# Mamba decay rows and their selection matrix: 64 contraction rows against 128, the added rows zero

## What is computed

```python
def _ssd_chunk(state, xs, A):
    x, dt, Bc, Cc = xs
    Q = x.shape[1]
    causal = jnp.tril(jnp.ones((Q, Q), dtype=bool))
    a = jnp.cumsum(dt * A, axis=1)
    seg = jnp.where(causal[None, :, :, None, None], a[:, :, None] - a[:, None, :], -jnp.inf)
    w = jnp.einsum('btgn,bsgn->btsg', Cc, Bc)[..., None] * jnp.exp(seg) * dt[:, None]
    y = jnp.einsum('btsgh,bsghp->btghp', w, x) + ...
```

## Time and profile before

| | |
|---|---|
| median of 3 runs | 1443.24 us (1440.71 to 1446.42) |
| span of the profiled execution, first to last instruction | 1436.6 us |
| own time of the profiled execution beside its span | not recorded |
| TensorE busy | 1412.7 us, 98% |
| VectorE busy | 1013.4 us, 71% |
| ScalarE busy | 719.4 us, 50% |
| GpSimd busy | 85.1 us, 6% |
| mean granted TensorE clock | 0.995 |
| DMA | 337.41 MB, 235 GB/s |

### The profile page before, as it was taken

One profiled execution on the slowest core, in us unless ns is written; L12 is line 12 of the kernel. 1 busy time (PEld: TensorE's weight loads), 2 busy tenths in 40 slices (PEclk: granted clock), 3 DMA queues, 4 the chain that ended last, 5 costly groups with the idle time before them and its releaser, 6 DMA issues.

```text
span 1436.6 us, 18540 instructions
## 1 busy us (share of the span) xinstructions
PE 1412.7 (98%) x7578; PEld 1205.4 (84%) x7578; DVE 1013.4 (71%) x1278; ACT 719.4 (50%) x931; POOL 85.1 (6%) x112
## 2 busy tenths in 40 slices
PE   9999999998999999999999999999999999999997
PEld 8788888987888878888789978788888799999886
DVE  5887776987977769777767965678746544653865
ACT  5544456456544365434566676554345645545433
POOL 1000001001000010000100352100000100000000
PEclk9999999999999999999999999999999999999999
DMA  9887865855978849887544412488755454445542
GB/s 384 358 335 296 334 227 192 320 187 201 390 295 314 311 151 347 308 322 300 201 147 164 175 60 88 176 333 337 282 194 201 147 194 174 147 164 189 186 153 116
DMA packets 51396, 337.41 MB, mean 235 GB/s; under 512 B 6720, under 2 KB 9584, under 8 KB 11376
## 3 DMA queue, kind: packets, MB, share of 16 engines
q1 hardware_dynamic: 51312, 336.23, 62.8%
HBM read 335.12 MB, written 1.09 MB: 234 GB/s over the span
## 4 chain that ended last, share of the span: by engine, by line
PE 87%; DVE 5%; ACT 3%; DMA 2%; issue 1%; POOL 1%; SPq 0%; ACTq 0%; POOLq 0%; DVEq 0%
PE ps L1010 84%; DMA raw<-units 2%; PE ps L1228 1%; DVE wlo L1642 1%; DVE hf L2056 1%; ACT whi L537 1%; PE ps L1119 1%; DVE M L1652 0%; ACT hf L618 0%; POOL base L457 0%; PE ps L1491 0%; POOL ssx L458 0%; DVE xlo L1717 0%; DVE wlo L1647 0%; ACT hf L612 0%
## 5 line engine op out<-in xcount | busy, mean ns | idle before, releaser
L1642 DVE TENSOR_TENSOR wlo<-raw,whi 128x2048 fp32r<-128x2048 f32 x212 | 485.4, 2294 | 206.6 <-ACT whi L537 206.3
L1010 PE MATMUL ps<-whi,xhi 128*128 128x512 f32 x1432 | 568.7, 397 | 7.5 <-DVE wlo L1647 1.7
L1010 PE MATMUL ps<-whi,xlo 128*128 128x512 f32 x1432 | 558.7, 390 | 0.0
L1010 PE MATMUL ps<-wlo,xhi 128*128 128x512 f32 x1432 | 558.5, 390 | 0.0
L537 ACT ACTIVATE whi<-raw 128x2048 fp32r<-128x2048 f32 x218 | 416.7, 1914 | 157.5 <-DMA raw<-units 157.5
L1010 PEld LDWEIGHTS ps<-whi,xhi 128*128 128x128 f32 x1432 | 269.3, 188 | 69.7 <-issue 5.3
L1010 PEld LDWEIGHTS ps<-whi,xlo 128*128 128x128 f32 x1432 | 269.1, 188 | 57.8
L1010 PEld LDWEIGHTS ps<-wlo,xhi 128*128 128x128 f32 x1432 | 269.5, 188 | 52.7 <-issue 0.2
L1010 PE MATMUL ps<-xhi,whi 128*128 128x256 f32 x704 | 202.7, 288 | 0.0
L1010 PE MATMUL ps<-xhi,wlo 128*128 128x256 f32 x704 | 199.9, 284 | 0.0
L1010 PE MATMUL ps<-xlo,whi 128*128 128x256 f32 x704 | 199.8, 284 | 0.0
(11 more groups left out here) (238 smaller groups left out, 981.4 us busy)
## 6 DMA issues: line engine op xcount, KB each, us to landing
raw<-units SPq DMA_DIRECT2D x218, 1024.0 KB, 4.9
M<-ada_units SPq DMA_DIRECT2D x82, 1024.0 KB, 7.0
M<-units SPq DMA_DIRECT2D x10, 1024.0 KB, 5.0
gp<-gate_rows SPq DMA_DIRECT2D x7, 512.0 KB, 7.3
M<-cvec SPq DMA_DIRECT2D x2, 512.0 KB, 4.5
x<-x_in SPq DMA_DIRECT2D x1, 1024.0 KB, 6.0
ada_a<-ada_units SPq DMA_DIRECT2D x1, 1024.0 KB, 18.5
ada_b<-ada_units SPq DMA_DIRECT2D x1, 1024.0 KB, 22.4
```

Of the source, the lines that this page charges most:

```text
L1010: return pe.matmul(out, lhsT, rhs, start=start, stop=stop, skip_group_check=True)
L1642: dve.tensor_tensor(rest(u), landed(u), rounded(u).bitcast(F32), ALU.subtract).then_inc(w_lo, 1)
```

## The change

`sel` and `arows` get 128 partitions instead of 64. GpSimd sets both to zero at the start, behind its other constants, and each memset adds 1 to `const`, so that TensorE's and VectorE's waits go to 6. VectorE's writes into rows 0 to 63 stay as they are. The matmuls of `decay` take all 128 rows; rows 64 to 127 add zero. Lines behind 442 of the kernel move down by 2.

```diff
--- before.py
+++ after.py
@@ -124,8 +124,8 @@
         mask = sb("mask", [P, SEQ])
         ident16 = sb("ident16", [P, P], BF16)
         mask16 = sb("mask16", [P, P], BF16)
-        sel = sb("sel", [2 * H_MB, H_MB], F32R)
-        arows = sb("arows", [2 * H_MB, SEQ], F32R)
+        sel = sb("sel", [P, H_MB], F32R)
+        arows = sb("arows", [P, SEQ], F32R)
         ps = ctx.enter_context(nc.psum_tensor("ps", [P, 8, 512], F32))
 
         def m(off, *shape):
@@ -440,6 +440,8 @@
             step(pool.memset(mask[:, :], 0.0))
             pool.affine_select(out=mask[:, 0:P], in_=mask[:, 0:P], compare_op=ALU.is_ge, fill=NEG, base=0,
                                pattern=[[1, P]], channel_multiplier=-1).then_inc(S["const"], 1)
+            pool.memset(sel[:, :].bitcast(F32), 0.0).then_inc(S["const"], 1)
+            pool.memset(arows[:, :].bitcast(F32), 0.0).then_inc(S["const"], 1)
 
             taken = {}
 
@@ -1144,7 +1146,7 @@
 
             pe.wait_ge(S["const"], 1)
             keep_clock(7, 28)
-            pe.wait_ge(S["const"], 4)
+            pe.wait_ge(S["const"], 6)
             pe.wait_ge(S["rows_in"], 16)
             for a in range(4):
                 r = pe.transpose(ps[:, 6, a * P:(a + 1) * P], vrow[:, a, :], ident[:, :])
@@ -1407,7 +1409,7 @@
                         for j in range(2):
                             h = 2 * p + j
                             mm(ps[:, 2 + p % 2, j * SEQ:(j + 1) * SEQ],
-                               sel[:, h:h + 1].to_broadcast([2 * H_MB, P]), arows[:, :], start=(j == 0))
+                               sel[:, h:h + 1].to_broadcast([P, P]), arows[:, :], start=(j == 0))
                         masked(p, 0).then_inc(S["mb_ab"], 1)
 
                     def masked(p, t):
@@ -1941,7 +1943,7 @@
                         dve.scalar_tensor_tensor(out=e[:, SEQ:384], in0=q[:, P:SEQ], scalar=colm[:, 1, h:h + 1],
                                                  in1=mask[:, 0:P], op0=ALU.add, op1=ALU.min).then_inc(S["ml_arg"], 1)
 
-                    dve.wait_ge(S["const"], 4)
+                    dve.wait_ge(S["const"], 6)
                     for h in range(H_ML):
                         exponent(h)
                     lo(u0 + 10)
```

## The result

| | before | changed |
|---|---|---|
| median | 1440.35 us (8 runs) | 1437.19 us (8 runs) |
| lowest to highest | 1438.98 to 1446.42 | 1435.84 to 1438.75 |
| ratio | | 0.9968, 95% interval 0.9956 to 0.9981 |
| span of the profiled execution | 1436.6 us | 1434.1 us |
| its own time | not recorded | 1435.84 us, 1.7 above the span |

What follows compares the result with a forecast made beforehand. TensorE, busy nearly the whole span, was taken to bound the kernel only where it is last waited for: 0.27 + 0.60 + 0.90 + 0.30 = 2.07 us off 1443.24 gives 1441.2 us; own range 1439 to 1443.5, with rivals 1437.0 to 1445.6.

Steps and rivals of the forecast that it cites:

- The delay of a pair: Decay pair in the Mamba loop, first mask to heads: 0.77 us falls to 0.45 to 0.48, taken as 0.30 saved.
- No cost of more rows, of the memsets and of the waits: Zero rows priced at 0; two start memsets and longer waits covered, 0 taken, +0.62 us at most.
- The pairs on the path: Of 16 decay pairs, those where TensorE carries the chain were counted: 2.07 us out of 4.80.
- The term of 0.27 for the first two pairs: Two pairs at 808: would give 0.60, counted 0.27 because VectorE had been idle only that long.
- The 0.90 for 847 to 861: TensorE's path from 847.51 to 861.17: three pairs ahead of the mask matmul that frees ScalarE, 0.90 us.
- a longer wait near 847: Sign in the profile after: TensorE waits more for VectorE near 847, where three pairs gain 0.
- The 0.60 for 831 to 847: Two pairs between 831.02 and 839.59 gain 0.60 us; three more, up to 846.5, gain 0.
- a rival of 3.35 us on either side of the forecast: One more clock fall, 1444.5 us, chance 0.11; or the recorded fall near 875 absent, 1437.8 us, chance 0.07.
- The direction I argued: From 861 to 876 a faster TensorE stands still more, up to 0.3 us a turn, which could tip another clock fall.
- The base: Start from the runs' median of 1443.24 us, 6.6 us above the profiled span, that part taken as unchanged.
- What can be told from no change: Whole kernel: a measurement can tell about 0.5%, 7.2 us; faster 0.04, slower 0.02, the same 0.94.
- Heads after 875: Test of the path: heads starting over 3.5 us or under 1 us earlier would make the path wrong.

Runs made afterwards that it cites:

- the two without falls: Profiles of the kernel before and the changed kernel, each with small products added in three TensorE waits of the loop; ratios 0.9977 and 0.9966.
- r_before: The kernel before, unchanged, timed against itself and profiled a second time; ratio 1.0005.
- ten pairs: Against the kernel before, only the ten decay pairs predicted as covered take 128 rows, the other six keep 64; ratio 0.9999.
- two pairs: Against the kernel before, only the 4th and 5th of 16 decay pairs take 128 rows; ratio 1.0006.
- 96 rows: The changed kernel with decay matmuls reading 96 of the 128 rows; ratio 0.9973 against the kernel before.
- six pairs: Against the kernel before, only the 4th, 5th, 9th, 10th, 11th and 14th decay pairs take 128 rows; ratio 0.9975.
- row maximum too: The changed kernel with the mLSTM stage's eight 4-row matmuls also filled to 128 rows from a zeroed tile; ratio 0.9976 against before.
- products in the waits: Kernel before and changed kernel, each with small products of ones added in three TensorE waits of the loop; means 1438.9 and 1437.2 us.
- forty matmuls of 64 and of 128 rows: The kernel before with forty extra matmuls in a row at two places of the third gated MLP; medians 1459.3 (64 rows) and 1458.8 us (128).
- the burst with 64 changes: The kernel before with 64 extra matmuls in the third gated MLP, alternating 64 and 128 rows; 1470.55 us, against 1454.39 with all 128.

## Why the prediction was right or wrong

- **The delay of a pair** was right: 0.29 us predicted by the steps (0.30 taken), 0.77 to 0.48 measured. The rule of the Trainium skill, TensorE: Matmul & The Clock Gate, Part 3 (What overlaps and what doesn't), that a load overlaps only in another row group did not hold here: the 128-row load of the pair starts with the mask matmul of 128 rows ahead of it.
- **No cost of more rows, of the memsets and of the waits** was right: a ratio of 1.0008 for the memsets and waits alone, and steps of 0.12 us with 128 rows.
- **The pairs on the path** were right as a set, and too high by a fifth in the sum: 1.61 us in the two profiles, 1.67 in the two without falls and 1.7 ± 0.9 in their runs, against 2.07. The term of 0.27 for the first two pairs measured 0.00: VectorE's convolution carries the chain from 788 to 823 in the changed profile. The 0.90 for 847 to 861 measured 0.32. The sum let the other engines' instructions keep their length; they did not. VectorE's weights took 3.13 instead of 2.28 us beside GpSimd, and the heads that wait for VectorE gave back 0.70 us; I had named a longer wait near 847 (it grew from 0.33 to 0.73), not this one. The 0.60 for 831 to 847 measured 0.94, and the 0.4 too much is again VectorE (1.16 instead of 1.59), which I had not foreseen: that the sum of 2.07 is not further off is in part luck.
- **The step that failed is the clock.** The prediction took a fall as one event of the recorded run, put a rival of 3.35 us on either side of the forecast with 0.11 and 0.07, and entered 0 in the sum. Against that, the changed kernel's mean clock over 32 runs is 0.9961 and before's 0.9945; by the line of 1.0 us for each 0.001, about 1.6 of the 3.1 us of gain go with it. The direction I argued, that a faster TensorE stands still more and so loses clock, is refuted by the mean: the waits did grow, and the clock rose. What the fall comes from I had half right: the wait for VectorE ahead of 875.84 is one of the three whose filling removes it. The size of a fall was about right, 3.0 us by the offsets from 875.8 to 882.3 against 3.35.
- **The base** failed too. I took 6.6 us as the time outside the span. It is 1.7 to 1.8 in every profile whose own time is recorded (1435.84 against 1434.1), so the profiled execution of before took about 1438.4 us by estimate, less than any of the eight timed ones. The forecast started from a median of three runs, 1443.24, and the median of eight is 1440.35. Of the 4.0 us between the forecast of 1441.2 and the measured 1437.19, the base is 2.9 and the gain 1.1 (1.6 too little for the clock, 0.4 to 0.5 too much for the path). Even the forecast's own range, 1439 to 1443.5, leaves 1437.19 out.
- **What can be told from no change** was wrong. I held 0.5% for the least that can be told, with 0.94 for the case that nothing is. A change of 0.32% was told from none with 8 runs, and the interval is ±0.13%.
- **The signs.** Mask to heads, the matmuls near 280 ns, the turn of 3.2 us (855.54 to 858.75) and the longer waits near 847 and 865 came as said. Heads after 875 were to start 1 to 3.5 us earlier; they start 0.56 later, so by this sign the path was wrong. It was a bad sign rather than a bad path: the offset had +0.64 in it from earlier stages and 1.53 from the fall at 830.9, and neither had been allowed for.

What stays open: why filled rows on the path raise the mean clock at all. The means differ in good part by the runs with the lowest clocks. Of the 158 runs of the kernel before and of the variants whose 9th to 11th pairs keep 64 rows (`r_before`, memsets alone, ten pairs, two pairs), 38 have a mean clock of 0.992 or less; of the 68 runs with the pairs of the path filled (changed kernel, 96 rows, six pairs, row maximum too), 3 do; of the 24 with products in the waits, none. Without such runs the means of the two groups are 0.9954 and 0.9963 instead of 0.9942 and 0.9961. The one execution of these variants with so low a clock that was profiled, two pairs at 0.990, has the fall of 20.5 us, and so have the profiles with forty matmuls of 64 and of 128 rows, at 0.989 and 0.990. So a good part of what the clock gives may be that such long falls get rare; no profile of before itself caught one, and no run says why they would. That the delays themselves count as standing still would fit (the burst with 64 changes has a lower mean clock too, 0.9910 against 0.9942), but the run with two filled pairs, at 0.9933, does not fit it, and no run separates the delays from the shift of the waits behind them.

## What to carry to other kernels

Look at the start times where TensorE goes from one row count to another: if the weight load starts with its matmul, zero rows up to the full array buy back 0.15 to 0.2 us a change, but only where TensorE carries the chain. A gain on TensorE also shifts the other engines against each other: look whether their instructions keep their length. When two executions of one program differ by more than the change, read the granted clock of each before anything else, and ask for the mean over many runs. Short waits of TensorE in a loop of small matmuls can cost as much again through the clock (filling 2.6 us of waits took 2.3 and 2.7 us off the means), and in a single execution several times as much; cheap matmuls into unused PSUM take that back.

## What was not expected of the hardware

- A run of 4-row matmuls brings the granted clock to 0.50 although TensorE is busy all the time (13.7 us at both places); a run of 64-row ones doesn't.
- 96 contraction rows cost no change against 128 (0.48 us from mask to heads), 64 do (0.77).
- A change of row count costs 0.19 us between matmuls of 512 columns, and 0.15 between those of 256.
- A fall of the clock may last 20.5 us while TensorE is fully busy (867.6 to 888.1), and cost over 7 us, more than this whole change gives. A fall of 3.4 us at 265 cost nothing in the end.
- VectorE's instruction of 128x2048 took 3.13 us instead of 2.28 where GpSimd was at work as it began.
